# Two weight loads issued before eighteen state stores, and a shorter wait for one of them

## What is computed

```python
x = x + 0.5 * swiglu(rmsnorm(x, ffn1_norm), ffn1_w_gate, ffn1_w_up, ffn1_w_down)   # 1024 -> 2816 -> 1024
p = rmsnorm(x, mix_norm) @ w_in                       # conv inputs, q, k, v, o and the gates
a_out = group_norm(bg * causal_conv3(cg * x_in))      # 512 channels
hm, C, n, m = mlstm(q, k, v, gates, C0, n0, m0)       # 4 heads, states C (64x128), n (64), m
x = x + concat(a_out, norm(hm) * sigmoid(o)) @ w_out  # the output projection, 1024 x 1024
x = x + 0.5 * swiglu(rmsnorm(x, ffn2_norm), ffn2_w_gate, ffn2_w_up, ffn2_w_down)
y = rmsnorm(x, final_norm)                            # returned with the new conv and mLSTM states
```

## Time and profile before

| | |
|---|---|
| three runs | 2111.6, 2114.56, 2118.52 us (median 2114.56) |
| the profiled execution's own time | 2109.08 us |
| its span, first to last instruction | 2107.3 us |
| mean granted PE clock over the span | 0.984 |
| PE busy | 2040.7 us, 97% of the span |
| DVE, ACT, POOL busy | 922.9, 508.3, 101.8 us |

### The profile page before, as it was taken

The page is one execution under the profiler, slowest core; times in us unless marked ns, Lnnn a source line. Parts: engine busy times, 40 slices in busy tenths (PEclk is TensorE's granted clock), DMA queues, the critical chain, the costliest instruction groups (busy, mean ns, idle before and its releaser), DMA issues. The chain is left out here.

```text
span 2107.3 us, 31398 instructions
## 1 busy us (share of the span) xinstructions
PE 2040.7 (97%) x12657; PEld 2012.4 (95%) x12657; DVE 922.9 (44%) x1562; ACT 508.3 (24%) x890; POOL 101.8 (5%) x144
## 2 busy tenths in 40 slices
PE   7999999999999998999999889999999999999997
PEld 6999999999999998999999789999999999999996
DVE  5433333343234347412666647534323432333347
ACT  5212111211011124232343423321111111112123
POOL 2000000000000022000000011100000000000012
PEclk9999999999999999999999899999999999999998
DMA  7011101110111011311012130111011110111002
GB/s 213 21 41 60 60 20 40 60 60 20 40 60 60 21 56 41 81 51 29 23 30 67 66 96 21 41 61 60 24 35 60 60 51 23 46 60 60 0 1 83
DMA packets 144179, 105.11 MB, mean 50 GB/s; under 512 B 6376, under 2 KB 136248, under 8 KB 144120
## 3 DMA queue, kind: packets, MB, share of 16 engines
q1 hardware_dynamic: 143976, 103.77, 16.1%
q10 hardware_dynamic: 144, 0.52, 0.1%
HBM read 95.36 MB, written 8.92 MB: 49 GB/s over the span
## 5 line engine op out<-in xcount | busy, mean ns | idle before, releaser
L220 PE MATMUL bank<-in_hi,w_hi 128*128 128x352 f32 x2256 | 740.5, 328 | 19.0 <-DVE in_lo L1062 7.5
L226 PE MATMUL bank<-in_hi,w_lo 128*128 128x352 f32 x2256 | 730.2, 324 | 0.0
L225 PE MATMUL bank<-in_lo,w_hi 128*128 128x352 f32 x2256 | 728.6, 323 | 0.0
L220 PEld LDWEIGHTS bank<-in_hi,w_hi 128*128 128x128 f32 x2256 | 427.8, 190 | 23.6 <-issue 9.2
L225 PEld LDWEIGHTS bank<-in_lo,w_hi 128*128 128x128 f32 x2256 | 429.6, 190 | 1.1
L226 PEld LDWEIGHTS bank<-in_hi,w_lo 128*128 128x128 f32 x2256 | 427.5, 190 | 0.0
L403 DVE TENSOR_TENSOR ffn_hidden<-ffn_silu,bank 128x352 f32<-128x352 f32 x132 | 68.8, 521 | 669.8 <-PE bank L226 590.4
L220 PE MATMUL bank<-ffn_hidden_hi,ffn_w_down 128*128 128x352 f32 x1056 | 343.0, 325 | 2.0 <-DVE vectors L775 0.7
L414 DVE SCALAR_TENSOR_TENSOR x<-bank,x 128x352 f32<-128x352 f32 x528 | 266.7, 524 | 161.8 <-PE bank L226 110.8
L226 PE MATMUL bank<-ffn_hidden_hi,ffn_w_down 128*128 128x352 f32 x924 | 298.0, 323 | 0.0
L225 PE MATMUL bank<-ffn_hidden_lo,ffn_w_down 128*128 128x352 f32 x924 | 297.6, 322 | 0.0
(11 more groups left out here) (221 smaller groups left out, 1661.3 us busy)
## 6 DMA issues: line engine op xcount, KB each, us to landing
raw<-in_ffn_w_gate SPq DMA_DIRECT2D x44, 512.0 KB, 4.0
ffn_raw_more<-in_ffn_w_down SPq DMA_DIRECT2D x44, 512.0 KB, 5.3
raw<-in_w_in SPq DMA_DIRECT2D x24, 512.0 KB, 3.8
raw<-in_ffn_w_up SPq DMA_DIRECT2D x22, 512.0 KB, 5.0
ffn_raw_more<-in_ffn_w_up SPq DMA_DIRECT2D x22, 512.0 KB, 5.2
x_parked<-x SPq DMA_DIRECT2D x3, 1408.0 KB, 5.8
x<-x_parked SPq DMA_DIRECT2D x3, 1408.0 KB, 9.8
raw<-in_w_out SPq DMA_DIRECT2D x8, 512.0 KB, 3.7
```

What stands on the lines that cost most here:

```text
L220: pe.matmul(out, w_hi, in_hi, start=first, stop=False)
L225: pe.matmul(out, w_hi, in_lo, start=False, stop=False)
L226: return pe.matmul(out, w_lo, in_hi, start=False, stop=last)
```

## The change

The loads of tiles 6 and 7 are issued right after those of tiles 3 to 5, before the wait for the last state update and before the eighteen state stores. ACT's high half of tile 6 waits for `o.mix_low` at 18, the first two splits of block 2, instead of 24, all of them; the high half of tile 7 keeps the wait for 24.

```diff
-            for d in range(3, 6):
+            for d in range(3, KT):
                 o.load(sp, d)
             sp.wait_ge(s.state_added, GROUPS)
...
                 sp.dma_start(m_, m_out[:, which:which + 1]).then_inc(s.stored, 16)
                 n += 2 * HEADS + 1
-            for d in range(6, KT):
-                o.load(sp, d)
             sp.wait_ge(s.lines_ready, 1)
...
     @block.scalar
     def _(act):
+        act.wait_ge(o.mix_low, BLOCKS * KT - KT + 2)
+        o.w_high(act, 6)
         act.wait_ge(o.mix_low, BLOCKS * KT)
-        o.w_high(act, 6)
         o.w_high(act, 7)
```

## The result

| | before | after |
|---|---|---|
| median of six runs | 2113.43 us (2110.64 to 2118.52) | 2099.38 us (2098.79 to 2104.07) |
| ratio, 95% interval | | 0.9935 (0.992 to 0.995) |
| the profiled execution, own time | 2109.08 us | 2099.46 us |
| its span, mean granted clock | 2107.3 us, 0.984 | 2097.6 us, 0.986 |

The changed kernel is faster by 14 us in the medians and by 9.6 us between the two profiled executions. For the profiled execution the working gave 2100.1 us, and the profiled one took 2099.46.

The account below looks back on a forecast made before the run. PE, busy 97% of the span, was taken as the bound, leaving only waits and clock: 6.3 us of wait plus 2.6 of clock, together 9.0, from 2114.56 to 2105.6 us; range 2100.5 to 2112.5.

Parts of the forecast that it names:

- The loads: SP's loads of tiles 6 and 7: issued at 1219.3 and 1220.5 us, landing after 3.7, at 1223.0 and 1224.2.
- The halves: Tile 6: ACT's high half from 1225.5 to 1226.6 us, DVE's low half until 1229.9, leaving 1.1 us of slack.
- The sum at the seam: PE at tile 6: the wait for `w_last` vanishes, 6.3 us, and the low clock after it, 2.6; together 9.0 us.
- Rival 1: Before tile 6: load still takes 10.8 us to land, 1.4 us wait stays; gain 7.6 us, time 2107.0; chance 0.09.
- Rival 2: PE's clock: the wait goes, but low clock elsewhere eats the 2.6 us; gain 6.3 us, time 2108.3; chance 0.08.
- Rival 3: PE at tile 6: held by something the view of waits does not name; gain 0, time 2114.6 us; chance 0.08.
- POOL's wait: PE's 3.0 us wait for POOL's sum of squares moves along whole; its clock loss, about 1.6 us, could vary.
- The stores: SP's eighteen issues run from 1220.9 to about 1232.0 us, the wait for landings ends at about 1240.6; cost nothing.
- Rival 4: ACT at L279: second SwiGLU's tiles land later than 1287.9 us, making the kernel slower, about 2122 us; chance 0.03.
- The rule on the shared interface: DVE's low half of tile 7, contending with POOL for SBUF, might take 3.0 us, ending at 1233.2, before 1234.95.

Follow-up runs that it names:

- the late loads: Changed kernel with the loads of tiles 6 and 7 waiting for the conv lines, no store ahead of them: 2106.45 us median of 4 runs, ratio 0.9958.
- The filled pause: Kernel before, with 38 matmuls into an unused bank between tiles 5 and 6 of block 0: 2108.56 us median of 12 runs, ratio 0.9988.
- tile 3 early: Changed kernel with both halves of tile 3 made right after those of tile 2, before block 1's splits: 2103.8 us median of 7 runs.
- the loads alone: Changed kernel, but ACT waits for all 24 splits before tile 6's high half, as before: 2104.16 us median of 5 runs, ratio 0.9959.
- without n: Kernel before without the eight stores of n (64 values of 4 bytes each): 2101.17 us median of 4 runs, ratio 0.9945.
- without C: Kernel before without the eight stores of C (64 x 512 bytes each): 2111.01 us median of 10 runs, ratio 0.9982.

## Why the prediction was right in its steps and wrong in its number

**The loads.** Forecast: issued at 1219.3 and 1220.5, landed within 4 us. Right for the first load (issued at 1219.23, landed after 3.8 us), too short for the second (5.2 us), and right in what matters, that each is in before ACT asks for it (tile 6 at 1225.4, tile 7 at 1228.0). The prediction counted two things as late, the issue and the way. By the experiments, and the one step worked out from them under the late loads, only the way mattered, and what makes it slow, which the prediction did not name, are the eight stores of 4-byte values.

**The halves.** Forecast for the high half of tile 6 1225.5, measured 1225.42; for its low half's end 1229.9, measured 1229.75; slack 1.1 us, measured 1.15. The shorter wait on ACT was costed at nothing, and both experiments on it alone show nothing.

**The sum at the seam.** Forecast 6.3 + 2.6 = 9.0 us; measured 94.8 - 85.8 = 9.0 us in the first pair, and the same in every later profile. The filled pause divides it: 2.6 us for the clock, and the other 6.4 for the wait (0.5 of them because the load came that much sooner in that execution, 5.9 left to the changed kernel). Rivals 1, 2 and 3 fall with this.

**POOL's wait.** It moved along whole (3.04 us before, 3.00 after). Its low clock, for which 1.6 us either way had been allowed, was gone in the changed kernel's three profiles, though not in the one with tile 3 early. By the last column of the table a profile without it is 0.4 us shorter on the mean. Between the first two profiles the projection starts 0.1 us sooner, the seam is 9.0 shorter and the rest 0.4 (2084.25 to 2074.74 at the piece at L198): 9.5 of the 9.6 us are accounted for.

**The stores.** The eighteen issues ran from 1220.78 to 1232.65, 0.7 us longer than worked out, but the wait for their landings ended at 1243.67 and not at 1240.6: 9.9 us after the last issue instead of 5.5. ACT still met its tile at 1287.74 without a wait. Rival 4 falls; its margin was 34 us on paper and some 30 in fact.

**The rule on the shared interface.** The low half of tile 7 took 1.21 us, although POOL worked beside it; in the kernels with the loads alone and without n it took 1.41. The traces show a difference in order: in the first case POOL's add began 0.13 us after DVE, in the other two POOL's copy had begun 0.15 and 0.14 us before it. None of them comes near the 3.0 us that had been allowed, and none reaches PE.

**The step that failed** is the last: "The profiled execution took 2109.08 us and would take 2100.1. The three runs' median is 5.5 us above it, 2114.56, and from there I get 2105.6 us", with a range of 3 us for a median. The offset of 5.5 us was carried over as if it belonged to the kernel; in the first six runs of the changed kernel the median lay 0.1 us below the profiled execution. It belongs to the runs: the projection starts anywhere from 1202.5 to 1210.8 us in twelve profiles, by how the low clock falls out in the mixer. The profile before had been one of the early ones, at 1203. Five of the changed kernel's first six runs took 2099 us, which is the level of its early profile, and in its second set, with the same program, three of six took 2106.5 to 2107.2. So both numbers owe something to luck: the 2100.1 came within 0.6 us because both first profiles reached the projection at 1203, and the median of the changed kernel fell outside the range because five of its six runs were early ones too. Its second set, with a median of 2105.26, lay 0.3 us from the forecast. The range should have come down to the profiled execution's own 2100.1 less 1 to 2 us.

Over all, the kernel before has a mean of 2112.8 us (70 runs, standard error 0.4) and the changed one 2101.5 us (18 runs, 0.7): 11.3 us less, give or take 1.6 at 95% if the runs are taken as independent. Set by set, against the runs of the kernel before beside them, the means differ by 13.7, 10.1 and 12.7 us. The profiles account for 9.5. Part of the rest may be chance in the mixer again; whether the change has a further share, which no profile showed, stays open.

## What to carry to other kernels

When a load is late, look at what stands ahead of it in its queue and at its landing time, not only at its issue: eight stores of 64 single values held a 512 KB load up by 10 us, while 256 KB in rows of 512 B did not. Put loads that an engine will wait for ahead of such stores; making the stores wider was not tried. And before a profiled execution's gain is carried over to a median, look at how far the kernel's own runs spread and where the profiled one lies among them. Span times mean clock, averaged over many runs, helps to tell the two causes apart: it fell from 2073.1 to 2067.6 us when the wait went, and hardly moved with the low clock in the mixer. It does not see a gain in clock: with the pause filled, which gave 2.6 us of clock back, it was 2074.5.

## What the runs showed of the hardware that was not expected

- A 512 KB load landed 13.7 us after its issue behind eight stores of 64 values of 4 bytes, and 3.5 us after it behind eight of 64 rows of 512 B. Counted from the first store's issue that is 20.1 and 9.9 us.
- PE's clock after a short pause is not the same each time. After POOL's wait of 3.0 us the first two matmuls (L132) took 1.54 us, at the low level, in six of the twelve profiles and 0.86 us in the six others; after the 3.16 us before tile 6 in the late loads it stayed at 1.00, after the 4.30 us without C it fell (0.71 between 1240 and 1244 us).
- The work up to the projection, the same in all these kernels, took up to 8.3 us longer in one execution than in another (1202.5 to 1210.8 us), with a mean clock of 0.95 down to 0.93 between 940 and 1200 us. Why the clock falls differently there was not looked into.
